# One stationary for high and low value columns in the second attention of a two-block kernel

## The chip, the cores and the metric

The kernel runs on one core of one Trainium2 chip. The time is the device time of one execution in microseconds, of which the median of several is taken. In the profile PE is TensorE (PEld its weight loads), DVE VectorE, ACT ScalarE, POOL GpSimd, SP the engine whose queue issues the DMAs. Shapes are written as partitions times free length, 128x512.

## The reference

Two blocks run one after the other on x of 512 tokens and 1024 features, all in float32. The first has a convolution branch, a stick-breaking attention and a feed-forward part. The second, in which the change lies, is this:

```python
h = rms_norm(x, norm_g)
mq, mk, mv, mg, dq, dk, dv, dg = split(h @ w_in)        # 8 standard heads of 64, 4 differential heads of 2 x 64
m_out = softmax(mq mk / 8 - slope * dist, causal) @ mv  # one per standard head, blocks of 256 keys, top 3: all of 512
m_out = m_out * silu(mg)
a = softmax(q1 k1) - lam * softmax(q2 k2)               # differential head, values of width 128
d_out = rms_norm(a @ dv, diff_subln) * 0.8 * silu(dg)
x = x + concat(m_out, d_out) @ w_out
```

## The kernel before

Activations are kept transposed, features on partitions and the 512 tokens along the free axis, in chunks of 128 features. Every float32 product is made of three matmuls (`products`, L461 to L465): each operand is split into a high part and a low part (`_hi`, `_lo`), and high by high, high by low and low by high are added in PSUM. ACT makes the high parts (a copy with rounding), DVE or POOL the low parts (a subtraction). POOL can't read PSUM, so what is split out of PSUM is DVE's. Weights arrive as 160 units of 128x1024 through four buffers `w_raw`; ACT makes `w_hi` (`split_unit`), POOL `w_lo` (`low_unit`), both double-buffered, and PE waits for `lo_ready`.

The order on every engine is written out by hand, and engines meet by semaphores alone, so an instruction that waits holds all that is behind it on its engine. The second attention goes through eight chunks c of 128 features: even c are differential heads, odd c are two standard heads (head 0 and head 1 of the chunk, of 64 features each). Each loop takes an even c with the odd c + 1. On PE (L1066 to L1098) one round has, around the change: `values2(c + 1, 0)`, five eighths of the gate tile of chunk c + 2 (`gate_part`), `values2(c + 1, 1)`, `den_rows(c + 1)` (the softmax denominators brought to rows), the rest of the gate tile; then, for the next round, `transposes(c + 2)` (probabilities brought to keys on partitions), `value_transposes`, `scores2(c + 3, 0)`, `value_half` of the value unit after that, `scores2(c + 3, 1)`, `gate_half(c + 3, 0)` and so on.

What the steps wait for, and what they write:

- `values2` (L955) of a standard head multiplies the transposed probabilities `pt_hi`, `pt_lo` (128x1280, the causal part in four pieces of 512, 384, 256 and 128 columns) by `v2_hi`, `v2_lo`. These have 64 columns of one head, 64 of zeros (`gap_zeroed`) and 64 of the other, so that each head fills its own 64 rows of `OUT_BANK` and both heads add up into one tile: 12 matmuls a head.
- `high_probs` (ACT, L1515) writes `pt_hi` from PSUM once the values of the head before are done; `low_probs` (DVE, L2234) writes `pt_lo`; then PE may go on with `values2`.
- `scores2(c, 1)` and `(c, 2)` wait for `biased` (DVE, L2173), which takes the scores out of PSUM; `exponentials` (ACT) follow it.
- `gated` (DVE, L2246) multiplies `OUT_BANK` by the gate into `att2[:, 1]` and frees the bank (`out_read`); `high_mixed` (ACT) and `mixed_low` (POOL) split the result into `b_hi`, `b_lo` for the output projection.
- `root` (DVE, L2275) is a Newton step and the norm of a differential head on `att2[:, 0]`, four instructions; `gated_out` (POOL) multiplies it by the gate.
- `value_half(c)` waits until `value_low(c - 1)` has emptied the bank of the values (`v2_lo_ready`); `gate_half(c, 0)` waits for `value_drain(c + 1)` (`vt_ready`) and for the low part of its weights; `gate_half(7, 0)`, which has no value chunk behind it, for `value_low(7)` and the low part of its weights.

Of the kernel before, what the change touches and what calls it, by code (L numbers as in the profile page):

```python
# [14 lines left out]
P = 128  # L15
T = 512
# [64 lines left out]
def two_layer_block(nc, xT, vecs, wstream, outT):  # L81
    with ExitStack() as ctx:
# [142 lines left out]
        v2_hi = put("v2_hi", [P, TB, P + 64], F32R)  # L225
        v2_lo = put("v2_lo", [P, TB, P + 64], F32R)
# [8 lines left out]
        assert at["sq_hi0"] + 4 * T * 4 <= at["vd_lo"] + 4 * T  # L235
# [62 lines left out]
        pool_held, gap_zeroed = sem("pool_held"), sem("gap_zeroed")  # L298
# [161 lines left out]
        def _(pe):  # L460
# [494 lines left out]
            def values2(c, head=0):  # L955
                tq = tq_of(c, head)
                at_col = 64 * half_of(c, head)
                if c >= KC:
                    return
                if is_diff(c):  # L960
                    v_hi2, v_lo2 = vd_hi, vd_lo
                else:
                    v_hi2, v_lo2 = v2_hi[:, :, at_col:at_col + P], v2_lo[:, :, at_col:at_col + P]
                if head == 0:
                    pe.wait_ge(v2_lo_ready, max(c + 1, 2))
                    if not is_diff(c):
                        pe.wait_ge(gap_zeroed, 2)
                        pe.wait_ge(dvar_ready, c // 2 + 1)
                    elif c:
                        pe.wait_ge(out_read, c // 2)  # L970
                pe.wait_ge(ptl_ready, tq + 1)
                for j in range(TB):
                    width = (TB - j) * P
                    w = slice(P_COL[j], P_COL[j] + width)
                    mm = products(ps[:, OUT_BANK, j * P:T], v_hi2[:, j, :], v_lo2[:, j, :],
                                  pt_hi[:, w], pt_lo[:, w], first=j == 0 and head == 0)
                mm.then_inc(av2_ready, 1)
# [143 lines left out]
        def _(act):  # L1121
# [366 lines left out]
            def stage_v2(c):  # L1488

                if c >= KC:  # L1490
                    return
                act.wait_ge(vt_done, c + 1)
                if c > 1:
                    act.wait_ge(av2_ready, tq_of(c - 2, 1) + 1 if not is_diff(c) else tq_of(c - 2) + 1)
                src = ps[:, v_bank(c), :].rearrange("p (b f) -> p b f", f=P)
                if is_diff(c):
                    act.activation(vd_hi[:, :, :], src, ACT.Copy).then_inc(v2_hi_ready, 1)
                else:
                    act.activation(by_heads(v2_hi[:, :, :])[:, :, 0:3:2, :], by_heads(src), ACT.Copy).then_inc(v2_hi_ready, 1)
# [45 lines left out]

            def high_mixed(c):
                if is_diff(c):
                    act.wait_ge(att2_final, c // 2 + 1)
                else:
                    act.wait_ge(out_read, c // 2 + 1)  # L1550
# [43 lines left out]
            for c in range(0, KC - 2, 2):  # L1594
                if c:
                    high_probs(c - 1, 1)
                    exponentials(c, 2)
                    high_mixed(c - 2)
                    split_unit(v_unit(c + 2))
                    split_unit(g_unit(c + 1))  # L1600
                    stage_v2(c + 1)
                high_probs(c)
                if c:
                    high_mixed(c - 1)
                exponentials(c + 1, 0)
                if c:
                    split_unit(v_unit(c + 3))
# [12 lines left out]
                stage_qk2(c + 3)  # L1620

            high_probs(KC - 3, 1)
            exponentials(KC - 2, 2)
            split_unit(g_unit(KC - 1))
            stage_v2(KC - 1)
            high_mixed(KC - 4)
            high_probs(KC - 2)
            high_mixed(KC - 3)
            exponentials(KC - 1, 0)
# [8 lines left out]
            gate_sigmoid(KC - 1)  # L1638
            high_probs(KC - 1, 1)
# [3 lines left out]
            split_out(4)  # L1643
            high_mixed(KC - 1)
# [5 lines left out]
        def _(dve):  # L1650
# [497 lines left out]
            def value_low(c):  # L2148
# [7 lines left out]
                else:  # L2156
                    low(by_heads(v2_lo[:, :, :])[:, :, 0:3:2, :], by_heads(src), by_heads(v2_hi[:, :, :])[:, :, 0:3:2, :]
                        ).then_inc(v2_lo_ready, 1)
# [87 lines left out]
            def gated(c):  # L2246

                dve.wait_ge(row2_used, c // 2 + 1)
                dve.wait_ge(av2_ready, tq_of(c, 1) + 1)
                if c > 1:  # L2250
                    dve.wait_ge(mixed_ready, c - 1)
                tt(att2[:, 1, :], ps[:, OUT_BANK, :], gate_e[:, chunk_of(c), :], ALU.mult).then_inc(out_read, 1)
# [65 lines left out]
            for c in range(0, KC, 2):  # L2318
# [41 lines left out]
        def _(pool):  # L2360
# [188 lines left out]

            def mixed_low(c):  # L2550
# [44 lines left out]
            pool.memset(v2_hi[:, :, 64:P].bitcast(F32), 0.0).then_inc(gap_zeroed, 1)  # L2595
            pool.memset(v2_lo[:, :, 64:P].bitcast(F32), 0.0).then_inc(gap_zeroed, 1)
# [4 lines left out]
            for c in range(0, KC - 2, 2):  # L2601
# [105 lines left out]
```

## Time and profile before

| what | value |
|---|---|
| median of 3 runs | 1017.64 us (1017.56 to 1017.75) |
| profiled execution | 1017.32 us |
| its span, first to last instruction | 1015.2 us |
| busy in the span: PE, DVE, POOL, ACT | 1002.7, 557.7, 502.3, 454.0 us |
| granted TensorE clock, mean | 1.00 |

The span is from the first to the last instruction; 2.1 us of the profiled execution lie around it. A busy time is the sum of the stretches in which an engine works. Matmuls are pipelined: one lasts 0.39 us and the next one starts after 0.23 us, so the distance between two starts is what a matmul costs.

### The profile page before, as it was taken

How to read it: one execution, taken by the hardware profiler on the slowest of the kernel's cores; microseconds unless marked ns; L12 is line 12 of the kernel's file. 1: busy time of each engine (PE TensorE's matmuls, PEld its weight loads, DVE VectorE, ACT ScalarE, POOL GpSimd, SP SyncE). 2: the span in 40 equal slices, each digit the busy share in tenths (PEclk: the TensorE clock that was granted, in tenths of full speed). 3: DMA queues.
4: the chain of work that ended last, by engine and by line, in shares of the span. 5: the costliest groups of instructions: out<-in, count | busy, mean ns of one | idle time of the engine just before them, and what ended most of it. 6: DMA issues, size and time to landing. Idle time of an engine off the chain costs nothing.

```text
span 1015.2 us, 13705 instructions
## 1 busy us (share of the span) xinstructions
PE 1002.7 (99%) x5051; PEld 836.2 (82%) x5051; DVE 557.7 (55%) x943; ACT 454.0 (45%) x682; POOL 502.3 (49%) x296
## 2 busy tenths in 40 slices
PE   9999999999999999999999999999999999999998
PEld 7888888788888988888888888889988778777787
DVE  6799897886633964434434410116714276675731
ACT  7222346888643533323323322233554347667630
POOL 4444365742347034444444365453377544755562
PEclk9999999999999999999999999999999999999999
DMA  7232222212144022222322333333132120111112
GB/s 258 83 104 97 92 83 71 75 63 83 65 184 146 21 93 94 103 92 94 103 92 94 103 104 104 104 122 107 43 104 82 63 84 22 64 63 43 42 63 83
DMA packets 26402, 91.11 MB, mean 90 GB/s; under 512 B 3056, under 2 KB 3184, under 8 KB 26224
## 3 DMA queue, kind: packets, MB, share of 16 engines
q1 hardware_dynamic: 26352, 90.42, 26.2%
q8 instruction: 34, 0.56, 0.2%
q14 instruction: 16, 0.13, 0.0%
HBM read 88.31 MB, written 2.10 MB: 89 GB/s over the span
## 4 chain that ended last, share of the span: by engine, by line
PE 87%; DVE 7%; ACT 3%; issue 1%; DMA 1%; POOL 0%; SPq 0%; DVEq 0%; ACTq 0%
PE ps L463 27%; PE ps L464 26%; PE ps L465 26%; PE ps L928 2%; PE ps L952 1%; DVE resid L2015 1%; PE ps L622 1%; DVE a_lo L1666 1%; DMA w_raw<-weights 1%; DVE sq_x L1659 1%; DVE q_raw L1659 1%; DVE mix L1659 1%; DVE b_lo L1666 1%; ACT s L1510 0%; PE ps L638 0%
## 5 line engine op out<-in xcount | busy, mean ns | idle before, releaser
L2363 POOL TENSOR_TENSOR w_lo<-w_raw,w_hi 128x1024 fp32r<-128x1024 f32 x137 | 325.9, 2379 | 412.0 <-ACT w_hi L1129 359.2
L1129 ACT ACTIVATE w_hi<-w_raw 128x1024 fp32r<-128x1024 f32 x133 | 139.2, 1046 | 281.6 <-PE ps L465 281.6
L463 PE MATMUL ps<-a_hi,w_hi 128*128 128x512 f32 (+1 forms) x544 | 211.7, 389 | 4.2 <-DVE v_lo L1663 3.1
L465 PE MATMUL ps<-a_hi,w_lo 128*128 128x512 f32 (+1 forms) x544 | 207.0, 380 | 0.0
L464 PE MATMUL ps<-a_lo,w_hi 128*128 128x512 f32 (+1 forms) x544 | 206.9, 380 | 0.0
L463 PE MATMUL ps<-b_hi,w_hi 128*128 128x512 f32 x392 | 152.9, 390 | 0.0
L465 PE MATMUL ps<-b_hi,w_lo 128*128 128x512 f32 x392 | 152.6, 389 | 0.0
L464 PE MATMUL ps<-b_lo,w_hi 128*128 128x512 f32 x392 | 152.5, 389 | 0.0
L463 PEld LDWEIGHTS ps<-a_hi,w_hi 128*128 128x128 f32 x544 | 102.3, 188 | 27.3 <-DVE v_lo L1663 4.4
L465 PEld LDWEIGHTS ps<-a_hi,w_lo 128*128 128x128 f32 x544 | 102.3, 188 | 20.0
L464 PEld LDWEIGHTS ps<-a_lo,w_hi 128*128 128x128 f32 x544 | 102.4, 188 | 18.3 <-issue 0.2
L463 PEld LDWEIGHTS ps<-b_hi,w_hi 128*128 128x128 f32 x392 | 73.6, 188 | 15.2
L465 PEld LDWEIGHTS ps<-b_hi,w_lo 128*128 128x128 f32 x392 | 73.6, 188 | 15.2
L464 PEld LDWEIGHTS ps<-b_lo,w_hi 128*128 128x128 f32 x392 | 73.6, 188 | 15.1
L1743 DVE SCALAR_TENSOR_TENSOR ps<-u_pad,vec,ps 128x512 f32<-128x512 f32 x112 | 75.4, 750 | 0.0
L463 PE MATMUL ps<-h_hi,w_hi 128*128 128x512 f32 (+1 forms) x186 | 69.2, 372 | 0.0
L464 PE MATMUL ps<-h_lo,w_hi 128*128 128x512 f32 (+1 forms) x186 | 69.0, 371 | 0.0
L465 PE MATMUL ps<-h_hi,w_lo 128*128 128x512 f32 (+1 forms) x186 | 69.0, 371 | 0.0
L1659 DVE TENSOR_TENSOR up_h<-up_u,up_s 128x512 f32<-128x512 f32 x22 | 51.2, 2330 | 21.2 <-ACT up_s L1389 21.1
L1659 DVE TENSOR_TENSOR up_u<-ps,scale_row 128x512 f32<-128x512 f32 x22 | 15.2, 690 | 82.0 <-PE ps L465 82.0
L1659 DVE TENSOR_TENSOR sq_f<-sq_f 128x512 f32<-128x512 f32 x13 | 12.5, 960 | 82.7 <-ACT sq_f L1413 82.0
L1510 ACT ACTIVATE s<-s,smax 128x384 f32<-128x384 f32 (+2 forms) x64 | 35.2, 552 | 16.9 <-DVE smax L2188 16.9
(339 smaller groups left out, 1729.0 us busy)
## 6 DMA issues: line engine op xcount, KB each, us to landing
w_raw<-weights SPq DMA_DIRECT2D x156, 512.0 KB, 3.2
resid<-x_t SPq DMA_DIRECT2D x8, 256.0 KB, 6.7
w_raw<-weights SPq DMA_DIRECT2D x8, 256.0 KB, 6.8
resid<-x_t SPq DMA_DIRECT2D x1, 2048.0 KB, 8.7
out_t<-out_sb SPq DMA_DIRECT2D x8, 256.0 KB, 2.0
vec<-vecs SPq DMA_DIRECT2D x1, 220.0 KB, 7.1
vec<-vecs SPq DMA_DIRECT2D x1, 4.0 KB, 1.8
```

What stands on the lines that cost most here:

```text
L463: pe.matmul(out, s_hi, m_hi, start=first, stop=False, skip_group_check=True)
L464: pe.matmul(out, s_hi, m_lo, start=False, stop=False, skip_group_check=True)
L465: return pe.matmul(out, s_lo, m_hi, start=False, stop=last, skip_group_check=True)
L622: pe.matmul(z_of(h)[:, o:o + (b + 1) * P], q[r, tok], k[r, keys], start=b != 0 and t == 0, stop=False, skip_group_check=True)
L928: mm = pe.matmul(scores_of(part, head, b), q2[rows, tok], k2[rows, keys], start=n == 0 and t == 0, stop=False, skip_group_check=True)
L952: mm = pe.transpose(psf[:, o:o + P], s2[:, head, src:src + P], ident[:, :])
L1129: act.activation(w_hi[:, k % 2, 0:width], w_raw[:, k, 0:width], ACT.Copy).then_inc(hi_ready, 1)
L1510: e = act.activation(s2[:, head, w], s2[:, head, w], ACT.Exp, scale=-1.0, bias=smax[:, head, b:b + 1], accum_out=den[:, kind_of(c), half_o ...
L1659: return dve.tensor_tensor(out, in0, in1, op)
L1666: return dve.scalar_tensor_tensor(out=out, in0=in0, scalar=scale, in1=high.bitcast(F32), op0=ALU.mult, op1=ALU.subtract)
L1743: V.do(dve.scalar_tensor_tensor(out=acc if k == TAPS - 1 else part, in0=src, scalar=w, in1=part, op0=ALU.mult, op1=ALU.add))
L2363: pool.tensor_tensor(w_lo[:, k % 2, 0:width], w_raw[:, k, 0:width], w_hi[:, k % 2, 0:width].bitcast(F32), ALU.subtract).then_inc(lo_ready, 1)
```

## The change

For standard heads `v2_hi` and `v2_lo` become `v2_parts`, four groups of 64 columns: high part of head 0, its low part, low part of head 1, its high part. Two neighbouring groups are one stationary of 128 columns, multiplied by `pt_hi` and by `pt_lo`: 8 matmuls a head, the product of the high columns in 64 rows of the bank and that of the low columns in the other 64. The halves then have to be added, for each head by itself: ACT copies the high half into `att2[:, 1]` (`out_copy`), DVE adds the low half out of PSUM (`head_add`), and only then may the other head start its accumulation (`head_added`). The gate product (`gated`) moves from DVE to POOL, but for the last chunk (`last_gated`). `root` moves on DVE from ahead of `biased(c + 2, 2)` to the end of the round. On ACT, `exponentials(c, 2)` goes ahead of `high_probs`, `stage_qk2(c + 1)` behind it, and `high_mixed` further down. On POOL, `gated(c + 1)` stands ahead of `low_unit(g_unit(c + 3))`, `gated_out(c)` moves behind that, and the zeroing of the gaps is gone.

```diff
-        v2_hi = put("v2_hi", [P, TB, P + 64], F32R)
-        v2_lo = put("v2_lo", [P, TB, P + 64], F32R)
+        v2_parts = put("v2_parts", [P, TB, 4, 64], F32R)
...
             def values2(c, head=0):
...
                 if head == 0:
                     pe.wait_ge(v2_lo_ready, max(c + 1, 2))
                     if not is_diff(c):
-                        pe.wait_ge(gap_zeroed, 2)
                         pe.wait_ge(dvar_ready, c // 2 + 1)
                     elif c:
                         pe.wait_ge(out_read, c // 2)
+                else:
+                    pe.wait_ge(head_added, c // 2 + 1)
                 pe.wait_ge(ptl_ready, tq + 1)
+                part = 2 * half_of(c, head)
                 for j in range(TB):
...
+                    if is_diff(c):
+                        mm = products(out, vd_hi[:, j, :], vd_lo[:, j, :], pt_hi[:, w], pt_lo[:, w], first=j == 0)
+                    else:
+                        values = v2_parts[:, j, part:part + 2, :].rearrange("p a f -> p (a f)")
+                        pe.matmul(out, values, pt_hi[:, w], start=j == 0, stop=False, skip_group_check=True)
+                        mm = pe.matmul(out, values, pt_lo[:, w], start=False, stop=j == TB - 1, skip_group_check=True)
...
+            def out_copy(c, head):
+
+                rows = slice(64 * half_of(c, head), 64 * half_of(c, head) + 64)
+                act.wait_ge(av2_ready, tq_of(c, head) + 1)
+                if head == 0 and c > 1:
+                    act.wait_ge(mixed_ready, c - 1)
+                act.activation(att2[rows, 1, :], ps[rows, OUT_BANK, :], ACT.Copy).then_inc(head_copied, 1)
...
             for c in range(0, KC - 2, 2):
                 if c:
+                    exponentials(c, 2)
+                    out_copy(c - 1, 0)
                     high_probs(c - 1, 1)
-                    exponentials(c, 2)
-                    high_mixed(c - 2)
+                    stage_qk2(c + 1)
                     split_unit(v_unit(c + 2))
+                    out_copy(c - 1, 1)
                     split_unit(g_unit(c + 1))
                     stage_v2(c + 1)
                 high_probs(c)
-                if c:
-                    high_mixed(c - 1)
                 exponentials(c + 1, 0)
                 if c:
+                    high_mixed(c - 2)
+                    high_mixed(c - 1)
                     split_unit(v_unit(c + 3))
...
                 exponentials(c + 2, 1)
-                stage_qk2(c + 3)
...
             gate_sigmoid(KC - 1)
+            out_copy(KC - 1, 0)
             high_probs(KC - 1, 1)
...
             split_out(4)
+            out_copy(KC - 1, 1)
             high_mixed(KC - 1)
...
+            def head_add(c, head):
...
+                high, small_ = 64 * half_of(c, head), 64 - 64 * half_of(c, head)
+                dve.wait_ge(head_copied, 2 * (c // 2) + head + 1)
+                tt(att2[high:high + 64, 1, :], att2[high:high + 64, 1, :], ps[small_:small_ + 64, OUT_BANK, :], ALU.add
+                   ).then_inc(out_read if head else head_added, 1)
...
                 value_drain(c + 3)
-                root(c)
+                if c + 2 == KC:
+                    root(c)
                 biased(c + 2, 2)
+                head_add(c + 1, 0)
+                joined(c + 2, (3,))
                 low_probs(c + 1, 1)
-                joined(c + 2, (3, 2, 0, 1))
+                joined(c + 2, (2, 0, 1))
                 gate_row(c + 1)
                 gate2_drain(c + 2)
                 slopes(c + 3)
                 value_low(c + 3)
+                head_add(c + 1, 1)
                 if c + 2 < KC:
-                    gated(c + 1)
-            gated(KC - 1)
+                    root(c)
+            last_gated(KC - 1)
...
+            def gated(c):
+
+                pool.wait_ge(row2_used, c // 2 + 1)
+                pool.wait_ge(out_read, c // 2 + 1)
+                pool.tensor_tensor(att2[:, 1, :], att2[:, 1, :], gate_e[:, chunk_of(c), :], ALU.mult).then_inc(gated_ready, 1)
...
                 gate_silu(c)
-                gated_out(c)
                 pool.wait_ge(p2_joined, c // 2 + 2)
                 stage_qk(c + 3)
                 if c + 4 < KC:
                     low_unit(v_unit(c + 4))
+                gated(c + 1)
                 low_unit(g_unit(c + 3))
+                gated_out(c)
                 mixed_low(c)
```

## Rows read from the trace of the kernel before

**Rows 1.** The page, part 1: busy time and share of the span.
```profile
PE 1002.7 (99%) x5051; PEld 836.2 (82%) x5051; DVE 557.7 (55%) x943; ACT 454.0 (45%) x682; POOL 502.3 (49%) x296
```
**Rows 2.** PE's longest wait: total us, times, longest us.
```profile
PE ps L463 <- DVE v_lo L1663: 3.1, 3, 1.0
```
**Rows 3.** Timeline of PE, first round: start us, us, instruction, count.
```profile
853.82 0.50 PE L463 MATMUL ps<-pt_hi,v_hi 128*128 128x512 f32 x1
...
855.80 0.45 PE L463 MATMUL ps<-a_hi,w_hi 128*128 128x512 f32 x1
...
859.28 0.39 PE L463 MATMUL ps<-pt_hi,v_hi 128*128 128x512 f32 x1
...
861.13 0.62 PE L984 MATMUL ps<-ident,rx_m 128*128 128x128 f32 x4
```
**Rows 4.** Timeline of PE, first attention, one head and what follows.
```profile
156.95 0.39 PE L656 MATMUL ps<-pa_hi,v_parts 128*128 128x512 f32 x1
...
158.16 0.44 PE L463 MATMUL ps<-a_hi,w_hi 128*128 128x512 f32 x1
```
**Rows 5.** Timelines of ACT and DVE, first round, and two groups by form.
```profile
856.06 1.24 ACT L1522 ACTIVATE pt_hi<-ps 128x1280 fp32r<-128x1280 f32 x1 [0.69 <-PE ps L465]
...
857.33 1.49 DVE L1663 TENSOR_TENSOR pt_lo<-ps,pt_hi 128x1280 fp32r<-128x1280 f32 x1
...
859.20 1.94 DVE L2205 SCALAR_TENSOR_TENSOR s<-s,fac 128x512 f32<-128x512 f32 x4
...
L1219 ACT ACTIVATE b_hi<-ps 64x512 fp32r<-64x512 f32 x8 | 4.7, 588 | 0.6 <-PE ps L657 0.3
...
L1659 DVE TENSOR_TENSOR b_lo<-ps,b_lo 64x512 fp32r<-64x512 f32 x8 | 5.5, 689 | 0.3
```
**Rows 6.** Timelines of POOL and DVE, first round, after the second head.
```profile
861.22 0.19 POOL L2519 TENSOR_TENSOR small<-small 128x1 f32<-128x1 f32 x1 [3.11 <-DVE s L2205]
...
864.00 4.91 POOL L2363 TENSOR_TENSOR w_lo<-w_raw,w_hi 128x1024 fp32r<-128x1024 f32 x2
...
864.49 2.18 DVE L1655 TENSOR_SCALAR bias<-dist,small 128x512 f32<-128x512 f32 x1
...
866.59 0.68 DVE L1663 TENSOR_TENSOR v_lo<-ps,v_hi 128x512 fp32r<-128x512 f32 x1
```
**Rows 7.** Timelines of DVE and POOL: `root`, first and last, and who waits.
```profile
853.99 0.68 DVE L1659 TENSOR_TENSOR d_sq<-d_y 128x512 f32<-128x512 f32 x1
...
855.97 0.69 DVE L2285 SCALAR_TENSOR_TENSOR att<-d_sq,d_y 128x512 f32<-128x512 f32 x1
...
856.81 1.30 POOL L2548 TENSOR_TENSOR att<-att,gate_e 128x512 f32<-128x512 f32 x1 [5.96 <-DVE att L2285]
```
**Rows 8.** Timelines of DVE and POOL at the start of the kernel.
```profile
11.37 7.97 DVE L1666 SCALAR_TENSOR_TENSOR a_lo<-resid,vec,a_hi 128x512 fp32r<-128x512 f32 x5 [1.05 <-ACT a_hi L1152]
...
13.86 3.22 POOL L2395 TENSOR_TENSOR wf_lo<-w_raw,wf_hi 128x512 fp32r<-128x512 f32 x2 [0.18 <-POOL wf_lo L2395]
```
**Rows 9.** Timelines of DVE and PE, first round, before the gate tile.
```profile
867.80 0.68 DVE L2188 CUSTOM_DVE_ANT_0 s<-ps,bias_h 128x512 f32<-128x512 f32 x1
...
873.10 0.69 DVE L1659 TENSOR_TENSOR v_t<-ps,scale_row 128x512 f32<-128x512 f32 x1 [2.59 <-PE ps L465]
...
873.99 0.50 PE L463 MATMUL ps<-a_hi,w_hi 128*128 128x512 f32 x1
```
**Rows 10.** Timelines of POOL and PE, third round: gate weights of chunk 7.
```profile
946.64 2.37 POOL L2363 TENSOR_TENSOR w_lo<-w_raw,w_hi 128x1024 fp32r<-128x1024 f32 x1
...
949.96 0.50 PE L463 MATMUL ps<-a_hi,w_hi 128*128 128x512 f32 x1 [1.02 <-DVE v_lo L1663]
```
**Rows 11.** PE at both ends: timeline, then window with busy times and PEclk.
```profile
1.63 4.18 PE L579 MATMUL ps<-a_lo,neg_ones 128*128 128x512 f32 x9 [1.63 <-POOL neg_ones L2373]
...
7.52 1.07 PE L592 MATMUL ps<-a_lo,wf_hi 128*128 128x512 f32 x4
...
1012.00:1015.20 3.20, 0.00 (x0) 0.00 (x0) 0.69 (x1) 0.00 (x0) 0.00 (x0) 0.88 0.21 82
```

More of the change, by code:

```diff
@@ L297, in two_layer_block @@
             sem("drs_ready"), sem("d_final"), sem("att2_final"), sem("mixed_ready"))
-        pool_held, gap_zeroed = sem("pool_held"), sem("gap_zeroed")
+        pool_held, head_added, gated_ready = sem("pool_held"), sem("head_added"), sem("gated_ready")
+        head_copied = sem("head_copied")
         first_done, first_sq, first_acc, first_drained = (
@@ L970, in values2 @@
                         pe.wait_ge(out_read, c // 2)
+                else:
+                    pe.wait_ge(head_added, c // 2 + 1)
                 pe.wait_ge(ptl_ready, tq + 1)
+                part = 2 * half_of(c, head)
                 for j in range(TB):
[L973 to L976, printed above, removed]
+                    w = slice(P_COL[j], P_COL[j] + (TB - j) * P)
+                    out = ps[:, OUT_BANK, j * P:T]
+                    if is_diff(c):
[4 more added lines that the diff above has]
+                        mm = pe.matmul(out, values, pt_lo[:, w], start=False, stop=j == TB - 1, skip_group_check=True)
                 mm.then_inc(av2_ready, 1)
@@ L1498, in stage_v2 @@
                 else:
-                    act.activation(by_heads(v2_hi[:, :, :])[:, :, 0:3:2, :], by_heads(src), ACT.Copy).then_inc(v2_hi_ready, 1)
+                    act.activation(v2_parts[:, :, 0:4:3, :], by_heads(src), ACT.Copy).then_inc(v2_hi_ready, 1)
             def exponentials(c, part):
@@ L1619, in _ @@
                 exponentials(c + 2, 1)
-                stage_qk2(c + 3)
+            exponentials(KC - 2, 2)
+            out_copy(KC - 3, 0)
             high_probs(KC - 3, 1)
-            exponentials(KC - 2, 2)
+            stage_qk2(KC - 1)
+            out_copy(KC - 3, 1)
             split_unit(g_unit(KC - 1))
             stage_v2(KC - 1)
+            high_probs(KC - 2)
+            exponentials(KC - 1, 0)
             high_mixed(KC - 4)
-            high_probs(KC - 2)
             high_mixed(KC - 3)
-            exponentials(KC - 1, 0)
             split_unit(U_W2)
@@ L2156, in value_low @@
                 else:
-                    low(by_heads(v2_lo[:, :, :])[:, :, 0:3:2, :], by_heads(src), by_heads(v2_hi[:, :, :])[:, :, 0:3:2, :]
-                        ).then_inc(v2_lo_ready, 1)
+                    low(v2_parts[:, :, 1:3, :], by_heads(src), v2_parts[:, :, 0:4:3, :]).then_inc(v2_lo_ready, 1)
             def slopes(c):
@@ L2244, in gate2_drain, with last_gated @@
                 tt(gate_g[:, chunk_of(c), :], ps[:, GATE_BANK, :], scale_row[:, :], ALU.mult).then_inc(g_drained, 1)
-            def gated(c):
+            def head_add(c, head):
+                if c >= KC:
+                    return
+                high, small_ = 64 * half_of(c, head), 64 - 64 * half_of(c, head)
+                dve.wait_ge(head_copied, 2 * (c // 2) + head + 1)
+                tt(att2[high:high + 64, 1, :], att2[high:high + 64, 1, :], ps[small_:small_ + 64, OUT_BANK, :], ALU.add
+                   ).then_inc(out_read if head else head_added, 1)
+            def last_gated(c):
+                dve.wait_ge(out_read, c // 2 + 1)
                 dve.wait_ge(row2_used, c // 2 + 1)
[L2249 to L2252, printed above, removed]
+                tt(att2[:, 1, :], att2[:, 1, :], gate_e[:, chunk_of(c), :], ALU.mult).then_inc(gated_ready, 1)
             def gate_row(c):
```

11 lines of the change are left out of this document (2 added, 9 removed).

## The prediction, made before the change was run

> **What bounds the kernel now.** I read the page's busy shares first: PE is busy for 99% of the span [rows 1], so only two things move the time, PE's own work and the moments at which PE stands still. Next I read PE's waits: the longest sum is three waits of 1.0 us on DVE's low part of the standard heads' values, `v_lo` [rows 2]. They are all in the second attention, one in each of its first three rounds. A round runs from the values of one standard chunk to those of the next and repeats every 41.3 us. Last I read the timelines of all engines in one such round, where the reader should see how much room lies between each step of ACT, DVE and POOL and the matmul that waits for it. Everything below is worked out on the first round (853.8 to 895.1 us), called A; the second, B, is the same; the third, C, has one weight unit less.
>
> **PE's saving.** `values2` of a standard head is now 12 matmuls in 1.85 us (859.28 to 861.13) [rows 3]. With high and low value columns in one stationary it is 8. The first attention already does that, with the same four widths: 156.95 to 158.16, 1.21 us [rows 4]. So 0.64 us a head, 5.1 us for eight heads, all on PE and so all on the path, if nothing new waits.
>
> **The second head's wait.** Between the two heads PE has 15 gate matmuls, 3.48 us (855.80 to 859.28) [rows 3]. Before, `high_probs` on ACT and `low_probs` on DVE ended at 858.82, 0.46 us ahead of need [rows 5]. After, head 0 ends on PE at 855.16. ACT has the moved exponentials behind it by 855.5, since `root` no longer stands before `biased(c+2, 2)` on DVE, so `out_copy` runs 855.5 to 856.06 (0.59 us for the like 64x512 copy) and `high_probs` until 857.2, as early as before. DVE first does `head_add` (0.69 us for the like 64x512 add, started at 856.10), then the fraction and block 3 of `joined`. Before, 1.87 us lie between the starts of `low_probs` and of the joins, 1.41 of them `low_probs`, so the fraction takes 0.46; block 3 adds 0.6. `low_probs` thus starts at 857.80 and ends at 859.28 [rows 5]. PE wants it at 858.64 and gets it at 859.34: 0.70 us of stall, plus 0.11 because the first matmul behind a wait starts its successor 0.34 us later, not 0.23. Head 1 starts 0.06 later than before and, being 0.64 shorter, leaves PE 0.45 us ahead of before at 860.68. Between bounds (no stall, and one `low_probs` more) I keep 0.8, three times; in the last chunk `out_chunks(1)` covers it.
>
> **The wait for `v_lo`.** POOL starts `stage_qk` when `joined` is done (861.14 before, 860.55 after), then the low part of the next value unit. DVE's `slopes`, at 2.18 us, end only when POOL's first 2.4 us subtraction has ended, and `v_lo` follows [rows 6]. All of this comes 0.57 us earlier: `value_half(c+3)` would start at 866.75 instead of 867.32.
>
> **The moved `root`.** Its four DVE instructions (853.99 to 856.66, 2.67 us) now run while POOL is idle: POOL waits for their result with 5.96 us idle [rows 7]. Moved behind `head_add(c+1, 1)` they start at 867.2, just when that add releases POOL's new `gated`, followed on POOL by `low_unit(g_unit(c+3))`. All have two inputs in SBUF. The trace shows what two such streams do to each other: between 11.37 and 19.34 five DVE instructions of this kind take 7.97 us, 1.59 each against 0.69 alone, and POOL's beside them 1.6 against 1.3 [rows 7, 8]. They take turns: DVE's ends about 0.6 us behind POOL's end, POOL's 1.15 behind DVE's. On A: first `root` instruction until 867.89; `gated` until 869.04; second until 869.6; weight subtraction (2.3) until 871.9; third until 872.5; fourth until 873.2. What is queued on DVE behind it is late: `biased(c+3, 0)` (1.23) until 874.4, `low_probs(c+2)` (1.41) until 875.8, `value_drain(c+4)` (0.69) until 876.5. PE wants the first at 872.3 for `scores2(c+3, 1)` and the last at 873.3 for `gate_half(c+3, 0)`; that half, which started at 873.99 before [rows 9], starts at 876.55. Net of all above: 2.56 us lost. B the same. The bounds of this term: POOL waits for the whole `root`, and PE then waits only for the gate weights until 873.6 (a gain of 0.4), and nothing better.
> The Trainium skill (SBUF — State Buffer, Who interferes with whom) has, in my words, the pair held for a whole instruction by whichever engine came first, and the order of issue decides. It names no turns; by it alone the order could also favour DVE's back-to-back instructions, which is the bound of 0.4 above.
>
> **Round C.** There is no value unit left, so `slopes` don't wait, but POOL's order now is `gated(5)`, then `low_unit(g_unit(7))`. Before, that low part was ready at 949.0, and PE started at 949.96 [rows 10]. Times of A hold here with 82.64 us added (867.32 is 949.96). After, `gated(5)` needs `head_add(5, 1)`, which DVE has behind `value_low(7)`: transposes until 947.4, ACT's high part until 948.1, low part until 948.8, add until 949.44. Then `root` and POOL take turns: `gated` until 951.2, the gate weights until 954.06. PE, free at 948.4, starts `gate_half(7, 0)` at 954.1: idle for 5.7 us and 4.14 us behind before. The least it can be, with no turn taken, is 948.8+0.6+1.3+2.4, 953.2: 3.2 us behind. This term needs no contention at all, only the order of POOL's queue.
>
> **Tail.** Chunk 7 keeps its two savings, 1.3 us. `last_gated` and `mixed_low(7)` have over 8 us of output matmuls above them. The `gap_zeroed` memsets and the wider `v2_parts` cost nothing: POOL waits there anyway.
>
> **Sum.** -2.56 -2.56 -4.14 +1.27 = 8.0 us longer. No price in it comes from a page.
>
> **The clock.** PE ran its first 13 matmuls of 512 columns at 0.43 us each, against 0.23 later, which is 1.2 and 2.4 GHz; in the last 3.2 us of the span, where PE is idle, the mean granted clock is 0.88, so it falls from full to half within them [rows 11]. PE's 5.7 us without a matmul in round C are longer, and I take it that PE then starts again at 1.2 GHz. The cost is from nothing (no fall) to 13 x 0.2 plus a remainder, 2.9 us; I take 2.2, nearer the row. Total 10.2. The profiled execution's span of 1015.2 becomes 1025.4; 2.1 us lie around the span (1017.32), so 1027.5, and from the median of 1017.64: **1027.8**.
> The Trainium skill (TensorE: Matmul & The Clock Gate, Part 1: The HAM clock gate) says in my words that an array left idle falls back to half clock and earns the full one again only by sustained work. It speaks against this change by way of round C; the trace agrees at both ends of the kernel.
>
> **Rivals.**
> - The clock holds through the idle stretch: +8.0, 1025.6. For it: all three present stalls of 1.0 us left the clock at 1.00.
> - DVE keeps its turn throughout `root`: A and B gain 0.3 each, C loses 5.5 since the gate weights are ready at 955.5, the tail gains 1.3: +3.6, with the clock 1023.4 at most. Against it: the turns in [rows 8].
> - No measurable change: no turns at all and only the least wait in C: 0.4+0.4-3.2+1.3 leaves 1.1 us of loss, 1018.7, if the clock holds too.
> - Faster: the change does what it is named for, with POOL's unit in C still ready by 949. Then the gain is 5.1 less 2.4 of second-head stalls plus 0.1 three times at `v_lo`: 1014.6, and 1012.5 without those stalls. It turns on whether `low_unit(g_unit(7))` is really queued behind `gated(5)`; the source says so.
>
> **How the numbers follow.** Forecast 0.45, clock holds 0.25, DVE keeps its turn 0.15, no measurable change 0.10, faster 0.05. A measurement of this kernel can tell about 0.2% (2 us) from no change. Slower by more is 0.85, within 0.10, faster 0.05. The range leaves out the last two and a little at the top, for a second slow stretch of the clock: 1020 to 1031.
>
> **What would show it.** Right: standard heads of 8 matmuls in about 1.2 us; PE waits of about 0.7 us ahead of the second head on `pt_lo`; in A and B waits of 1 to 2 us for `biased` and `v_t`, where now only `v_lo` stands; `root`'s instructions at up to 2.5 us; one wait of 5 to 6 us on POOL's `w_lo`, with half-clock matmuls behind it. Wrong: if no PE wait for `w_lo` appears in round C, the largest term is gone; if `root` runs at 0.7 us an instruction, A and B turn into small gains.

## The result, and the profile after

| what | value |
|---|---|
| before, beside the changed kernel | 1017.6 us (1017.31 to 1017.75) |
| changed kernel | 1032.76 us (1030.95 to 1033.05, 4 runs) |
| ratio | 1.0146 (95%: 1.0128 to 1.0163) |
| profiled execution after, its span | 1032.9 us, 1031.0 us |
| granted clock after, mean | 0.992 |

The change makes the kernel 1.5% slower. The forecast was 1027.8 us with a range up to 1031: the direction was right, the size too small by 5 us, and the range missed.

The page of the changed kernel, part 1 (busy us, share, instructions), answers to [rows 1]: PE has 32 instructions less and is busy for 97% instead of 99%. That it is busy longer all the same is the clock's doing: the kernel with POOL's other order below has the same 5019 instructions, no half clock in its profile, and PE busy for 998.9 us.

```profile
PE 1004.8 (97%) x5019; PEld 835.3 (81%) x5019; DVE 576.5 (56%) x948; ACT 458.5 (44%) x690; POOL 508.8 (49%) x297
```

PE's waits after (total us, times, longest us) take the place of the one line in [rows 2].

```profile
PE ps L463 <- POOL w_lo L2388: 5.8, 1, 5.8
PE ps L928 <- DVE smax L2202: 3.2, 2, 1.6
PE ps L463 <- DVE v_t L1674: 3.1, 2, 1.5
PE ps L976 <- DVE pt_lo L1678: 2.9, 3, 1.0
...
PE ps L463 <- DVE v_parts L1678: 1.6, 2, 0.8
```

16.6 us of waits stand where 3.1 stood. Their places are in PE's timeline, rounds A and C (start us, us, instruction, idle before and releaser).

```profile
859.54 0.47 PE L976 MATMUL ps<-pt_hi,v_parts 128*128 128x512 f32 x1 [0.97 <-DVE pt_lo L1678]
...
866.77 0.51 PE L463 MATMUL ps<-a_hi,w_hi 128*128 128x512 f32 x1 [0.76 <-DVE v_parts L1678]
...
874.13 0.44 PE L928 MATMUL ps<-k_hi,q_hi 64*128 64x384 f32 x2 [1.62 <-DVE smax L2202]
...
876.75 0.50 PE L463 MATMUL ps<-a_hi,w_hi 128*128 128x512 f32 x1 [1.55 <-DVE v_t L1674]
...
964.69 0.76 PE L463 MATMUL ps<-a_hi,w_hi 128*128 128x512 f32 x1 [5.83 <-POOL w_lo L2388]
```

DVE's timeline in round A shows `root` (L1674 `d_sq` to L2306), which [rows 7] had at 0.69 us an instruction, and what DVE does last before PE's next scores.

```profile
867.36 0.68 DVE L1674 TENSOR_TENSOR d_sq<-d_y 128x512 f32<-128x512 f32 x1
867.96 1.84 DVE L2300 SCALAR_TENSOR_TENSOR d_y<-att,small,d_y 128x512 f32<-128x512 f32 x1
869.72 2.87 DVE L2303 SCALAR_TENSOR_TENSOR d_sq<-d_sq,d_v 128x512 f32<-128x512 f32 x1
872.63 0.69 DVE L2306 SCALAR_TENSOR_TENSOR att<-d_sq,d_y 128x512 f32<-128x512 f32 x1
...
876.61 1.06 DVE L2230 SCALAR_TENSOR_TENSOR den<-den 128x4 f32<-128x4 f32 x1
877.71 2.63 DVE L2243 COPY rx_d<-den 128x512 f32<-128x512 f32 x1
```

POOL's timeline beside it:

```profile
867.58 1.67 POOL L2579 TENSOR_TENSOR att<-att,gate_e 128x512 f32<-128x512 f32 x1 [1.75 <-DVE att L1674]
869.22 2.84 POOL L2388 TENSOR_TENSOR w_lo<-w_raw,w_hi 128x1024 fp32r<-128x1024 f32 x1
...
877.70 2.37 POOL L2388 TENSOR_TENSOR w_lo<-w_raw,w_hi 128x1024 fp32r<-128x1024 f32 x1
```

The reader should lay the two side by side: the two long instructions of `root` end 0.5 to 0.6 us behind the POOL instruction that each of them met, the copy 0.3 us behind its own. The last pair, 877.70 and 877.71, is the one that the prediction did not have. The windows of the changed kernel (busy time with count for PE, PEld, DVE, ACT and POOL, then the granted clock, DMA share, GB/s) show the clock low in A, B and C:

```profile
878.00:880.00 2.00, 2.00 (x7) 1.52 (x6) 2.00 (x1) 0.00 (x0) 2.00 (x1) 0.50 0.01 4
...
924.00:926.00 2.00, 2.00 (x6) 1.52 (x6) 2.00 (x1) 0.00 (x0) 2.00 (x2) 0.50 0.00 0
...
966.00:968.00 2.00, 2.00 (x6) 1.52 (x6) 2.00 (x6) 1.40 (x4) 1.25 (x1) 0.50 0.58 231
```

It is at 1.2 GHz from 877.2 to 880.6, from 921.6 to 928.4 and from 962.5 to 969.3.

### The profile page after: what moved, and what is told of

The parts are those of the page before. It is cut to its first block, busy times and chain, and to the rows that moved or that the text cites. A ratio compares the mean times of both kernels' runs of the same rounds, so it can differ in the third digit from the quotient of the medians.

```text
span 1031.0 us, 13659 instructions
## 1 busy us (share of the span) xinstructions
PE 1004.8 (97%) x5019; PEld 835.3 (81%) x5019; DVE 576.5 (56%) x948; ACT 458.5 (44%) x690; POOL 508.8 (49%) x297
## 4 chain that ended last, share of the span: by engine, by line
PE 81%; DVE 11%; ACT 4%; issue 1%; POOL 1%; DMA 1%; SPq 0%; DVEq 0%; ACTq 0%; POOLq 0%
PE ps L463 25%; PE ps L464 24%; PE ps L465 24%; PE ps L928 1%; DVE resid L2030 1%; PE ps L952 1%; PE ps L622 1%; ACT s L1511 1%; DVE pt_lo L1678 1%; DVE a_lo L1681 1%; DVE s L2219 1%; DVE d_sq L2303 1%; DMA resid<-x_t 1%; DVE sq_x L1674 1%; DVE q_raw L1674 1%
## 5 line engine op out<-in xcount | busy, mean ns | idle before, releaser
L463 PE MATMUL ps<-a_hi,w_hi 128*128 128x512 f32 (+1 forms) x544 | 214.3, 394 | 11.6 <-POOL w_lo L2388 5.8
L465 PE MATMUL ps<-a_hi,w_lo 128*128 128x512 f32 (+1 forms) x544 | 209.4, 385 | 0.0
L464 PE MATMUL ps<-a_lo,w_hi 128*128 128x512 f32 (+1 forms) x544 | 209.2, 385 | 0.0
L1674 DVE TENSOR_TENSOR up_h<-up_u,up_s 128x512 f32<-128x512 f32 x22 | 51.3, 2330 | 21.2 <-ACT up_s L1390 21.1
L1674 DVE TENSOR_TENSOR up_u<-ps,scale_row 128x512 f32<-128x512 f32 x22 | 15.2, 690 | 82.0 <-PE ps L465 82.0
L1674 DVE TENSOR_TENSOR sq_f<-sq_f 128x512 f32<-128x512 f32 x13 | 12.5, 960 | 82.6 <-ACT sq_f L1414 82.0
```

Source lines behind the costliest of these rows:

```text
L463: pe.matmul(out, s_hi, m_hi, start=first, stop=False, skip_group_check=True)
L464: pe.matmul(out, s_hi, m_lo, start=False, stop=False, skip_group_check=True)
L465: return pe.matmul(out, s_lo, m_hi, start=False, stop=last, skip_group_check=True)
L1674: return dve.tensor_tensor(out, in0, in1, op)
```

## The experiments

The theory: POOL and DVE, meeting on operands in SBUF, delay `root` and what follows it (A, B); POOL's new order delays the gate weights (C); the clock falls behind those waits. The rivals were that the clock, one of the moves, or the separate heads alone made the loss. Each diff is against the changed kernel where nothing else is said; kernels of one group share their runs of before. The kernel before measured 1017.6 us beside the changed kernel and 1017.1 to 1017.2 beside the groups, so a difference to the changed kernel is sure to about half a microsecond. The prediction names the steps from the loop before; its `scores2(c + 3, 1)` is `scores2(c + 1, 1)` in the code of the next loop, and this section goes by the code.

### First group: one part at a time (before: 1017.12 us)

**POOL's order.** The gate weights go ahead of `gated`.

```diff
-                gated(c + 1)
                 low_unit(g_unit(c + 3))
+                gated(c + 1)
                 gated_out(c)
```

> The changed kernel with one swap on POOL: the low part of the gate weights of chunk c + 3 ahead of the gate product. Theory (POOL's order makes the longest wait, and turns with root the waits in rounds A and B): the 5.8 us wait for w_lo in round C is gone, 5.4 us, and the half-clock stretch behind it with it, 2.3 us. In A and B only one POOL instruction is left to take turns with root, which ends 1.5 us earlier, so the waits for smax and v_t together fall from 3.2 to about 1.7 us a round. Sum 10.7: about 1022, and down to 1018 if the clock then holds in A and B too. Rival (root's new place alone carries the loss, and PE would wait for v_parts and biased scores in round C as long): round C gains 1 us at most, about 1030.

Measured 1024.64 us (1023.53 to 1025.48), ratio 1.0074 (1.0057 to 1.0091): 8.1 us won back, the largest effect of one edit that keeps the computation as it is, but 2.6 less than expected. The wait for `w_lo` in C is gone; in its place stand 2.1 us for `smax` (total us, times, longest us):

```profile
PE ps L928 <- DVE smax L2202: 5.3, 5, 2.1
PE ps L463 <- DVE v_t L1674: 3.1, 2, 1.5
PE ps L976 <- DVE pt_lo L1678: 2.9, 3, 1.0
```

Of the five for `smax`, the two ahead of `scores2(c + 1, 1)` in A and B have fallen from 1.6 to 0.2 us, as expected, but the waits for `v_t` stay at 1.5, and two new ones of 1.34 and 1.35 us (at 879.77 and 924.12) stand ahead of `scores2(c + 1, 2)`, where the prediction has no wait. For `smax` and `v_t` together A and B thus still wait 3.1 us each, where 1.7 was expected; twice the difference is 2.8, about what is missing.

**`root` at its old place.**

```diff
                 value_drain(c + 3)
-                if c + 2 == KC:
-                    root(c)
+                root(c)
                 biased(c + 2, 2)
...
                 head_add(c + 1, 1)
-                if c + 2 < KC:
-                    root(c)
```

> The changed kernel with root at its old place on DVE in every round. Theory: the waits for smax and v_t (3.2 us a round in A and B) and the half-clock stretches behind them (1.7 and 2.8 us) go, but root's 2.7 us now stand ahead of biased(c + 2, 2), so that the exponentials, the copy of head 0 and low_probs come 2.4 us later and the wait ahead of the second head grows from 1.0 to 3.4 us in three rounds; round C keeps its wait for w_lo, 1.2 us shorter as nothing takes turns with POOL. Sum -6.4 -4.5 +7.2 -1.2: about 1028. Rival (the wait ahead of the second head has cover, so root costs nothing there): 1021.

Measured 1033.85 us (1032.38 to 1034.22), ratio 1.0161 (1.0144 to 1.0178): a miss by nearly 6 us. `root` then stands ahead of the first `head_add`, and the second head waits 3.5 us three times (timeline of PE, round A):

```profile
861.85 0.77 PE L976 MATMUL ps<-pt_hi,v_parts 128*128 128x512 f32 x1 [3.48 <-DVE pt_lo L1678]
```

The waits for `smax` and `v_t` are gone, as expected. What was not: the clock is at half from 860.5 to 867.3, from 908.3 to 911.7 and from 952.7 to 956.1, one stretch at each of these waits, and again at the 5.1 us for `w_lo`. Moving `root` was thus no mistake by itself: with the heads separated its old place costs as much as the new one.

**`root` left out.** In the first three rounds the norm of the differential heads is not computed, and a memset releases POOL in its place.

```diff
                 if c + 2 < KC:
-                    root(c)
+                    dve.wait_ge(drs_ready, c // 2 + 1)
+                    dve.memset(small[:, 25:26], 0.0).then_inc(d_final, 1)
```

> The changed kernel without root in rounds A, B and C: a tiny instruction gives its signal, and the norm of these three differential heads is left out of the computation. Theory: no wait for smax and v_t (6.3 us in sum), no half clock in A and B (4.5 us), the wait for w_lo 1.2 us shorter and its half clock kept: about 1020.8. Rival (the waits in A and B come from the longer chain through copy and add, not from root): within 2 us of the changed kernel, 1031 to 1033.

Measured 1021.21 us (1020.91 to 1021.98), ratio 1.0041 (1.0026 to 1.0055). This met the number. Without `root` neither the 1.6 and 1.5 us waits of A and B nor their half clock appear, and these remain:

```profile
PE ps L463 <- POOL w_lo L2389: 5.0, 1, 5.0
PE ps L976 <- DVE pt_lo L1678: 2.9, 3, 1.0
...
PE ps L463 <- DVE v_parts L1678: 1.6, 2, 0.8
```

The 5.0 us in C without any `root` beside POOL show that this term is the order of POOL's queue, as the prediction had it.

**The waits filled.** PE runs extra matmuls that nobody reads, 6 ahead of `scores2(c + 1, 1)` and 6 ahead of `gate_half(c + 1, 0)` in A and B, 22 ahead of the gate in C, so that it is never idle for long.

```diff
+            def filler(count, bank, seen):
+
+                pe.wait_ge(s2_biased, seen)
+                for _ in range(count):
+                    pe.matmul(ps[:, bank, :], a_hi[:, 0, 0:P], a_hi[:, 0, :], start=True, stop=True, skip_group_check=True)
...
+                    filler(6, 6, 8 * (c + 1))
                     scores2(c + 1, 1)
+                    filler(6, 5, 8 * (c + 1) + 2)
                     gate_half(c + 1, 0)
...
+                    if c:
+                        filler(22, 6, 8 * (c + 1))
                     gate_half(c + 1, 0)
```

> The changed kernel with matmuls of no use put where PE waits: 6 ahead of the second part of the scores and 6 ahead of the gate tile in A and B, 22 ahead of the gate tile in C, 0.23 us each and written to free banks. They take less time than the waits. Theory (the half-clock stretches are a cost of their own): the clock stays at 1.00 throughout and the time falls by 1.7 + 2.8 + 2.3 = 6.8 us, to about 1026. Rival (the half clock only falls into waits and costs nothing, or DVE's, ACT's and POOL's waits set the time): no change, 1032 to 1033.

Measured 1029.36 us (1029.13 to 1029.5), ratio 1.0119 (1.0102 to 1.0136). The clock stays at 1.00 and 3.4 us come back, half of what was expected. Most of the rest, 2.7 of 3.4 us, is in two waits that the half clock had hidden (timeline of PE):

```profile
880.96 0.39 PE L928 MATMUL ps<-k_hi,q_hi 64*128 64x256 f32 x2 [1.36 <-DVE smax L2212]
```

The same stands at 926.75. With the clock at full speed PE comes to `scores2(c + 1, 2)` before DVE has done the `biased` that it needs.

### Second group: the new wait, and a plan of my own (before: 1017.21 us)

**The copy behind `biased`.** Against the filled kernel, in chunks 2 and 4.

```diff
-                den_small(c)
-                den_spread(c)
+                if not 0 < c < KC - 2:
+                    den_small(c)
+                    den_spread(c)
                 biased(c + 1, 1)
                 if 0 < c < KC - 2:
+                    den_small(c)
+                    den_spread(c)
```

> The changed kernel with the filling matmuls of before (clock at 1.00), and on DVE the spread of the denominators behind biased(c + 1, 1) instead of ahead of it in the two middle rounds. Theory (the waits of 1.36 us for smax that appeared once the clock held come from the spread copy, 2.6 us long because POOL's subtraction holds it up): both waits go, 2.7 us faster than the filled kernel, about 1026.7. Rival (they come from root's lateness through biased itself): no change, 1029.4.

Measured 1027.03 us (1026.46 to 1027.67), ratio 1.0095 (1.0079 to 1.011): 2.3 us less, and both waits are gone. So `den_small` and the copy `den_spread`, 1.08 and 2.65 us long in the filled kernel, kept `biased` from being in time. They were moved together, and no run tells what each has by itself. Behind `biased` they take 2.12 and 0.81 us, and PE doesn't wait for them.

**Replanned.** The 8-matmul values stay, and what surrounds them is put elsewhere (cut to its core):

```diff
-                    gate_part(c + 2, 0, 5)
+                    gate_part(c + 2, 0, 6)
...
                 biased(c + 2, 2)
+                if c + 2 < KC:
+                    root(c)
                 head_add(c + 1, 0)
-                joined(c + 2, (3,))
                 low_probs(c + 1, 1)
-                joined(c + 2, (2, 0, 1))
+                joined(c + 2, (3, 2, 0, 1))
+                slopes(c + 3)
                 gate_row(c + 1)
                 gate2_drain(c + 2)
-                slopes(c + 3)
                 value_low(c + 3)
                 head_add(c + 1, 1)
-                if c + 2 < KC:
-                    root(c)
...
-                gated(c + 1)
                 low_unit(g_unit(c + 3))
+                gated(c + 1)
                 gated_out(c)
```

`root` here is its first half, two instructions; the second half goes ahead of `value_drain` in the next round, and `mixed_low` and `high_mixed` run later.

> The changed kernel with the same matmuls, replanned so that nothing takes turns: on POOL the gate weights ahead of the gate product and the mixed low part later; on DVE root in two halves, the first two instructions in the 1.4 us in which DVE waits for the copy of head 0, the last two behind low_probs of the next chunk while POOL is idle; low_probs ahead of all joins again; slopes ahead of gate_row, before POOL's subtractions start; six eighths of the gate tile between the heads; on ACT the mixed high parts behind the second exponentials. Theory (the matmul saving of 5.1 us is real and only the waits hide it): no wait ahead of the second head, at most 0.4 us for v_parts in each of three rounds, no wait for w_lo, clock at 1.00: -5.1 and up to -2 of the old 3.1, about 1010.5. Rival (copy and add between the heads can't be hidden): waits of about 1 us in three rounds stay, 1014 or more.

Measured 1015.64 us (1015.04 to 1017.3), ratio 0.9989 (0.998 to 0.9998): 17 us below the changed kernel, 5 above what I expected. Four of its 11 runs, 1016.9 to 1017.3 us, have a clock of 0.998. PE waits 0.9 us in all for `k_lo` and 0.8 us for `wo_lo`, and a new wait for weights had come up on POOL:

```profile
PE ps L463 <- POOL w_lo L2393: 4.4, 3, 1.5
```

**The split of the gate tile back to five.** Only `gate_part(c + 2, 0, 5)` again, against the replanned kernel.

> The replanned kernel with five eighths of the gate tile between the heads, as in both original kernels, 0.69 us less cover. Theory (the wait ahead of the second head is the end of low_probs against the end of the cover): a wait of 0.3 to 0.7 us ahead of the second head in three rounds, so 1 to 2 us slower than with six. Rival (copy and add, not the cover, decide): no difference.

Measured 1016.11 us (1015.59 to 1016.44), ratio 0.9987 (0.9978 to 0.9996). Against the replanned kernel that is 0.5 us more in the medians and less in the ratios, so this split decides nothing that can be told here. With five, the second head waits 0.39 us three times and the wait for `w_lo` is 1.26 instead of 1.46.

**The kernel before with `slopes` early.** Is the wait for `v_lo` of [rows 2] to be had without the change? Against the kernel before:

```diff
                 joined(c + 2, (3, 2, 0, 1))
+                slopes(c + 3)
                 gate_row(c + 1)
                 gate2_drain(c + 2)
-                slopes(c + 3)
```

> The kernel before with slopes ahead of gate_row on DVE and nothing else. Theory (its three waits of 1.0 us for v_lo come from slopes, held up by POOL's subtraction): the 2.18 us instruction falls to 0.5, the waits fall to 0.3 to 0.5 us each, 1.5 to 2.2 us faster, about 1015.3. Rival (v_lo waits for ACT's high part or for the transposes): no change.

Measured 1015.70 us (1015.31 to 1016.06), ratio 0.9984 (0.9975 to 0.9994). The three waits for `v_lo` fall from 1.0 to 0.5 us each. The timeline of DVE shows `slopes` at 0.48 us where [rows 6] has 2.18, since POOL isn't at its weights yet:

```profile
861.15 0.48 DVE L1655 TENSOR_SCALAR bias<-dist,small 128x512 f32<-128x512 f32 x1
```

### Third group and the last run (before: 1017.2 and 1017.11 us)

**A better plan.** Against the replanned kernel: POOL's value unit goes ahead of `stage_qk`, ACT's `split_unit` of it ahead of `out_copy`, and in A and B all of `root` sits behind the next round's `low_probs`, where POOL is idle. Not shown: on ACT `exponentials(c, 2)` goes behind `high_probs` again, and in the tail one output unit is split earlier on ACT and on POOL.

```diff
                 if c:
+                    if c + 2 < KC:
+                        root(c - 2)
                     root_end(c - 2)
...
-                if c + 2 < KC:
+                if c + 4 == KC:
                     root(c)
...
-                pool.wait_ge(p2_joined, c // 2 + 2)
-                stage_qk(c + 3)
                 if c + 4 < KC:
                     low_unit(v_unit(c + 4))
+                pool.wait_ge(p2_joined, c // 2 + 2)
+                stage_qk(c + 3)
```

> The replanned kernel, with its last waits taken away: the value unit's low part on POOL ahead of its wait for the joins (its high part on ACT ahead of the copy of head 0), root in one piece behind low_probs of the next chunk (in the last round its first half stays ahead of head_add), the exponentials behind high_probs again, and one output unit split earlier in the tail. Theory: the three waits of 1.46 us for w_lo and the one of 0.83 us in the tail go, what stays is at most 0.3 us a round ahead of the scores: 1015.6 less 4.4 and 0.8, about 1010.6. Rival (POOL's unit ahead of the joins takes turns with them, and the scores wait for k_lo instead): 1013 or more.

Measured 1014.52 us (1014.2 to 1016.43, 10 runs), ratio 0.9975 (0.9965 to 0.9984). Again some 4 us short of the hope: one wait of 1.5 us for `w_lo` stays, in C, and PE waits 1.13 and 1.14 us for `smax`, as in the filled kernel, and for the same reason. DVE's timeline of round A has all four instructions of `root` at 0.68 to 0.75 us now, and then:

```profile
872.47 0.93 DVE L2231 SCALAR_TENSOR_TENSOR den<-den 128x4 f32<-128x4 f32 x1
873.43 2.59 DVE L2244 COPY rx_d<-den 128x512 f32<-128x512 f32 x1
```

**POOL's order with the copy behind `biased`.** Both edits, in the changed kernel.

> The changed kernel with POOL's gate weights ahead of the gate product and, on DVE, the spread of the denominators behind biased(c + 1, 1) in the two middle rounds. Theory (two separate causes): the two waits of 1.35 us for smax that the first swap alone leaves go too, 1024.6 less 2.7, about 1021.9. Rival (the spread is late only because of POOL's old order): 1024.6.

Measured 1024.16 us (1022.86 to 1026.26), ratio 1.0075 (1.0057 to 1.0091), the same as for the order alone. The profile shows the two waits of 1.35 us gone, but the median is only 0.5 us below the order alone. The runs of this kernel spread over 3.4 us, all at a clock of 0.995 to 0.998, and its profile has a half-clock stretch from 959.4 to 962.8 that the other's has not. The two profiles tell more than the medians. From the second head in A to `value_half` in C is 95.93 us with the order alone (859.57 to 955.50) and 93.02 with both (859.94 to 952.96), 2.9 less, as expected. At the last matmul (1018.35 and 1017.41) only 0.9 us is left between the two, and the half-clock stretch lies in between. So the swap's gain is there, and the clock takes most of it back.

**A third matmul for each piece.** Against the better plan; the product of low by high is added twice, so the result is another one.

```diff
                         pe.matmul(out, values, pt_hi[:, w], start=j == 0, stop=False, skip_group_check=True)
+                        pe.matmul(out, values, pt_lo[:, w], start=False, stop=False, skip_group_check=True)
```

> The kernel of the last improvement with a third matmul for each piece of a standard head again (the low probabilities once more, so that this part of the result is changed), 12 instead of 8 a head. Theory (the saved matmuls are worth 0.64 us a head once nothing waits): 5.1 us slower than without, less what disappears into waits that are left, so 4.5 to 5.1. Rival (four of the twelve matmuls ran beside something else, or the replanning and not the saving makes the gain): under 2 us slower.

Measured 1019.29 us (1018.78 to 1019.52), ratio 1.0019 (1.001 to 1.0029): 4.8 us more. Giving the 32 matmuls back costs about what taking them out was forecast to save, 5.1 us for eight heads, once what surrounds them keeps up.

**The better plan with the copy behind `biased`.** The same swap of `den_small` and `den_spread` as above.

> The replanned kernel e8_best, with the rows of denominators (den_small, den_spread) moved behind biased(c + 1, 1) in chunks 2 and 4. In e8_best PE waits 1.13 and 1.14 us for smax ahead of scores2(c + 1, 2) while DVE's den_spread, 2.59 us instead of 0.43, runs beside POOL's subtraction of a whole weight unit. Theory (the long copy stands ahead of the biased that PE wants, and nothing else is late there): both waits go, 1014.5 becomes 1012.3 us in the executions whose clock holds (down to 1012.0), and the wait of 1.45 us for w_lo in round C stays. Rival (in the replanned order the denominators themselves are wanted at once): PE waits for rx_d instead, 1013.5 to 1015.

Measured 1012.04 us (1011.57 to 1013.18, 5 runs), ratio 0.9951 (0.9938 to 0.9965): close to the 1012.3 expected, 0.5% (5.1 us) faster than before and 20.7 us below the changed kernel. The kernel before can have 1.5 of these 5.1 us without the change, by `slopes` alone, so the change with its new plan is worth some 3.6 us against the better kernel before (the two were not run side by side). Both waits for `smax` are gone. DVE's timeline has `biased` from 872.4, and the copy behind it, at 0.80 us:

```profile
873.80 1.66 DVE L2231 SCALAR_TENSOR_TENSOR den<-den 128x4 f32<-128x4 f32 x1
875.50 0.80 DVE L2244 COPY rx_d<-den 128x512 f32<-128x512 f32 x1
```

The small instruction is now the one that is held. What is left of PE's waits in the rounds is mainly this one, in C:

```profile
PE ps L463 <- POOL w_lo L2399: 1.5, 1, 1.5
```

## Why the prediction came out as it did

**Right, step by step.** The second head starts late three times; `value_half` was forecast for 866.75 and started at 866.77, which is in part luck, since round A itself began 0.22 us early (853.60 instead of 853.82). The end of `root` was forecast for 873.2 and is 873.3; `scores2(c + 3, 1)` for 873.9 and is 874.13; `gate_half(3, 0)` for 876.55 and is 876.75. What the prediction said of the turns that DVE and POOL take, read from the start of the kernel [rows 7, 8], held in the round to 0.2 us. In C the wait is 5.83 us against 5.7. The saving on PE is real: the third matmul costs 4.8 us.

**The step that failed first: the list of what is late behind `root`.** The prediction followed DVE's queue through `biased`, `low_probs` and `value_drain`, and closed the round with "Net of all above: 2.56 us lost". It thus let the loss of a round stand at 2.56 from `gate_half(c + 3, 0)` on. Next in that queue come, in the names of the next loop, `den_small(c)`, `den_spread(c)` and `biased(c + 1, 1)`, for which PE waits again. With the clock held, in the filled kernel, rounds A and B cost 4.5 and 4.4 us each and not 2.56: between the first heads of successive rounds lie 45.81 and 45.72 us (853.43, 899.24, 944.96), where the kernel before has 41.32. In the kernel before DVE's timeline has the two small steps so:

```profile
873.71 0.15 DVE L2216 SCALAR_TENSOR_TENSOR den<-den 128x4 f32<-128x4 f32 x1
873.89 0.43 DVE L2229 COPY rx_d<-den 128x512 f32<-128x512 f32 x1
```

and POOL's timeline has its next subtraction:

```profile
874.29 2.41 POOL L2363 TENSOR_TENSOR w_lo<-w_raw,w_hi 128x1024 fp32r<-128x1024 f32 x1 [3.96 <-ACT w_hi L1129]
```

POOL begins only as the copy ends. After, both begin together (877.70 and 877.71), and the copy takes 2.63 us. The prediction had said of the moved instructions "All have two inputs in SBUF" and looked for no others, though `den_small` has them too and takes 1.06 us after instead of 0.15. In the filled kernel this wait costs 1.36 us twice, and the swap gave 2.3 us back.
The Trainium skill (SBUF — State Buffer, SBUF: two separate sides) says in my words that DVE also takes the port pair that it shares with POOL for an operation in a two-port mode, and it names the float32 copy from SBUF to SBUF as such a one. By that the step could have been foreseen, and the trace agrees: 0.43 us alone, 2.63 beside POOL.

**The second: the clock.** I priced one fall, behind the 5.7 us of C, and none in A and B, though I forecast waits of 1 to 2 us there; the only rows that I had on short waits were the three of 1.0 us that left the clock at 1.00. In A a wait of 1.62 us and one of 1.55 end 2.6 us apart, and half clock begins 0.4 us behind the second; B has the same two waits, and there it begins within the second (921.6, where PE starts again at 922.68). The filled kernel tells it apart. The last gate tile, `gate_half(7, 0)`, starts at 949.96 before, at 963.27 filled and at 964.69 after; the last matmul starts at 1011.61, 1023.86 and 1027.47. The rows, from the timelines of PE, two of the filled kernel and then the last matmul of the kernel before and of the changed one:

```profile
963.27 0.47 PE L463 MATMUL ps<-a_hi,w_hi 128*128 128x512 f32 x1 [0.70 <-POOL w_lo L2398]
...
1023.86 0.39 PE L465 MATMUL ps<-b_hi,wo_lo 128*128 128x512 f32 x1
...
1011.61 0.39 PE L465 MATMUL ps<-b_hi,wo_lo 128*128 128x512 f32 x1
...
1027.47 0.39 PE L465 MATMUL ps<-b_hi,wo_lo 128*128 128x512 f32 x1
```

So the falls of A and B cost 1.4 us net (964.69 - 963.27), small because the slow matmuls run while PE would have waited for `smax` anyway. The whole of the clock is 3.61 us at the last matmul (1027.47 - 1023.86), so the fall of C costs 3.61 - 1.42, that is 2.2 us. That is the very value that was forecast for it, but it was a pick between nothing and 2.9, so the exactness is luck.

**The sum again.** Before to after the last matmul is 15.9 us later. Forecast were 8.0 without the clock and 2.2 with it, 10.2. To that come the two waits for `smax`, 2.7, and the falls of A and B, 1.4. The remaining 1.5 lie, but for small items that cancel, in the distances within a round. From the start of the first head to that of the second is 5.94 us in A (853.60 to 859.54), where the forecast's times have 5.52: the copy and the add end when they were forecast to, though the round began 0.22 us early; `low_probs` starts at 857.91 instead of 857.80, and PE 0.15 us behind its end instead of 0.06. From the first head to the gate tile the loss is the same 0.4 us, in A and in B (23.15 and 23.16 us, forecast 22.73), and in C it is 0.6 (18.24, forecast 17.64). No run separates this last part further.

**The range.** It reached to "a second slow stretch of the clock" and nothing else. One missed wait in a round that occurs twice, with the clock of that round and 0.4 us more ahead of its second head, was outside it.

## What to carry to other kernels

When a step is moved to a place where another engine is busy, follow the queue behind it until the first instruction that is early again, not until the first wait that the bottleneck feels; and give every instruction on the way its duration beside the other engine, copies and tiny ones included. A saving on the bounding engine counts only as far as its suppliers keep up: here the same 5 us of saved matmuls ended as 15 us lost in one order of the queues and as 5 us gained in another, 1.5 of which didn't need the saving. A wait that is hidden under a slow clock comes out when the clock is mended, so cure both before judging either.

## What the runs showed of the chip

- In the changed kernel PE waits 1.6 us and then 1.55 us, 2.6 us apart by their ends, in A and in B. In A half clock begins 0.4 us behind the end of the second wait, in B already within it. The single waits of 1.0 us in the kernel before left the clock at 1.00. In between, the same waits come out both ways: with POOL's other order PE waits 0.77 us and then 2.13 us in C and keeps its clock in the profile, and with the copy behind `biased` added it waits 0.74 and 2.13 us there and falls to half 1.2 us later. In the profile of the better plan half clock begins at 949.2, behind a wait of 1.45 us. So the length of a wait alone doesn't tell here whether the clock falls.
- What the clock costs depends on what else is late: in C of the changed kernel it is low for 6.8 us, 2.2 of them while PE is idle anyway, and costs 2.2; in A and B it is low for 3.4 and 6.8 us and costs 1.4 together.
- Where the clock is granted varies between executions of one kernel. The better plan has runs of 1014.2 to 1014.65 us at a clock of 1.00, and of 1015.8 to 1016.4 at 0.998. The changed kernel's runs spread over 2.1 us, those with POOL's order and the copy moved over 3.4, those of the kernel before over at most 1.2 us in any group.
- An instruction of DVE on 128x4 elements, 0.15 us in the kernel before, takes 0.93 to 2.12 us where POOL's subtractions run beside it (0.93 in the better plan, 1.06 in the changed kernel, 1.66 in the last, 2.12 in the filled kernel with the swap). Its size is no measure of what it costs there.
